# Memory key projection with 512-column products, its weights two rows to a chunk, first loads in halves, and four products on a zeroed tile ahead of it

## What is computed

```python
def memory_kv(mem, norm_mem, wk, wv, k_norm):
    mn = rms_norm(mem, norm_mem)
    k = rms_norm((mn @ wk).reshape(B, N_MEM, X_HEADS, X_HD), k_norm)
    v = (mn @ wv).reshape(B, N_MEM, X_HEADS, X_HD)
    return k, v
```

## Time and profile before

| | us |
|---|---|
| median of 3 runs | 1373.4 (1371.75 to 1374.05) |
| the profiled execution's own time | 1376.92 |
| its span on the core | 1375.1 |
| PE, DVE, ACT, POOL busy in the span | 1339.6, 828.0, 612.3, 119.8 |

### The profile page before, as it was taken

One profiled execution on the slowest core, in us unless ns is written; L12 is line 12 of the kernel. 1 busy time (PEld: TensorE's weight loads), 2 busy tenths in 40 slices (PEclk: granted clock), 3 DMA queues, 4 the chain that ended last, 5 costly groups with the idle time before them and its releaser, 6 DMA issues.

```text
span 1375.1 us, 27283 instructions
## 1 busy us (share of the span) xinstructions
PE 1339.6 (97%) x10211; PEld 1309.1 (95%) x10211; DVE 828.0 (60%) x1256; ACT 612.3 (45%) x865; POOL 119.8 (9%) x165
## 2 busy tenths in 40 slices
PE   7999999989999999999999999999999999999999
PEld 7998989877999988999999999999999999999999
DVE  7767888767666557856544555544555544565443
ACT  7674656465544454544333334333333333343332
POOL 0040000111322215400000000000000000000000
PEclk9999999988999999999999999999999999999999
DMA  9686444754864963654555455554455544545553
GB/s 380 254 240 223 133 136 136 221 176 138 304 234 158 283 238 123 195 171 154 168 168 168 153 173 164 168 167 164 151 174 168 167 161 162 164 155 181 162 162 128
DMA packets 75277, 251.88 MB, mean 183 GB/s; under 512 B 8332, under 2 KB 17376, under 8 KB 74560
## 3 DMA queue, kind: packets, MB, share of 16 engines
q1 hardware_dynamic: 59184, 215.49, 47.1%
q0 software_dynamic: 15744, 35.07, 8.1%
q10 hardware_dynamic: 288, 0.48, 0.1%
HBM read 238.00 MB, written 13.63 MB: 183 GB/s over the span
## 4 chain that ended last, share of the span: by engine, by line
PE 78%; DVE 11%; ACT 5%; issue 4%; DMA 2%; SPq 0%; DVEq 0%; ACTq 0%
PE g L514 74%; DVE arena L1434 4%; PE m L514 3%; ACT arena L981 2%; DMA raw<-in_stream 2%; DVE wlo L1448 2%; DVE arena L1431 2%; ACT whi L999 1%; DVE a_lo L1434 1%; DVE b_lo L1434 0%; DVE small L1714 0%; ACT a_hi L981 0%; DMA arena<-in_memT 0%; DVE small L1431 0%; PE m L739 0%
## 5 line engine op out<-in xcount | busy, mean ns | idle before, releaser
L1448 DVE TENSOR_TENSOR wlo<-raw,whi 128x1024 fp32r<-128x1024 f32 x388 | 477.7, 1241 | 371.9 <-ACT whi L999 360.2
L999 ACT ACTIVATE whi<-raw 128x1024 fp32r<-128x1024 f32 x388 | 407.6, 1058 | 479.1 <-PE g L514 439.4
L514 PE MATMUL g<-a_hi,whi 128*128 128x288 f32 x1632 | 355.6, 299 | 0.9 <-ACT a_hi L981 0.9
L514 PE MATMUL g<-a_hi,wlo 128*128 128x288 f32 x1632 | 351.1, 296 | 0.0
L514 PE MATMUL g<-a_lo,whi 128*128 128x288 f32 x1632 | 349.8, 296 | 0.0
L514 PE MATMUL g<-b_hi,whi 128*128 128x288 f32 x1344 | 287.3, 295 | 2.8 <-DVE arena L1431 2.7
L514 PE MATMUL g<-b_hi,wlo 128*128 128x288 f32 x1344 | 288.7, 296 | 0.0
L514 PE MATMUL g<-b_lo,whi 128*128 128x288 f32 x1344 | 286.8, 295 | 0.0
L514 PEld LDWEIGHTS g<-a_hi,whi 128*128 128x128 f32 x1632 | 263.6, 189 | 7.8 <-issue 4.8
L514 PEld LDWEIGHTS g<-a_lo,whi 128*128 128x128 f32 x1632 | 263.4, 189 | 0.0
L514 PEld LDWEIGHTS g<-a_hi,wlo 128*128 128x128 f32 x1632 | 262.7, 189 | 0.0
(11 more groups left out here) (181 smaller groups left out, 722.9 us busy)
## 6 DMA issues: line engine op xcount, KB each, us to landing
raw<-in_stream SPq DMA_DIRECT2D x388, 512.0 KB, 3.5
arena<-in_state_C POOLq DMA_DIRECT2D x8, 512.0 KB, 6.9
out_s_C<-arena POOLq DMA_DIRECT2D x8, 512.0 KB, 3.4
arena<-in_kdT POOLq DMA_DIRECT2D x8, 512.0 KB, 17.1
arena<-in_cache_mem_v POOLq DMA_DIRECT2D x8, 512.0 KB, 7.9
arena<-in_xT SPq DMA_DIRECT2D x4, 576.0 KB, 8.5
arena<-in_xT POOLq DMA_DIRECT2D x1, 2304.0 KB, 10.3
arena<-in_memT SPq DMA_DIRECT2D x4, 512.0 KB, 7.2
```

Of the source, the lines that this page charges most:

```text
L514: return pe.matmul(out, lhsT, rhs, start=start, stop=stop, skip_group_check=True)
L999: act.activation(whi[:, s], raw[:, s], ACT.Copy).then_inc(sem["hi_done"], 1)
L1448: dve.tensor_tensor(wlo[:, s], raw[:, s], f32(whi[:, s]), SUB).then_inc(sem["chunk_split"], 1)
```

## The change

`weight_stream` gives the eight memory key chunks another shape: chunk c holds two tiles of 128 rows (kt = 2c, 2c+1) with all 512 columns. `mem_chunk` runs them: two row tiles, three products, two tiles of 128 tokens, so 12 matmuls of 512 columns; the sums of all eight chunks stay in G[2] and G[3]. memT is loaded in eighths, five of them ahead of chunk 4 and three behind chunks 4 to 6. Chunk 0 is loaded and split in two halves with signals of their own. `mem_prep` and `x_prep` move to other chunks: `mem_prep` pairs beside chunks 0 to 4, `x_prep` pairs beside chunks 3 to 10. `warm` runs four products of `rstd` with itself, which DVE has just set to zero. DVE empties the memory keys after beside[7], in four copies of 256 columns. `chunk` itself, with its wait for `tile_out`, is not edited. In the diff a line "..." marks what is left out.

```diff
     every = range(0, D, CK * P)
-    out = tiles(w["wk_x"][0], every, range(0, XW, CW))
+    out = [w["wk_x"][0][r:r + 2 * P].reshape(2, P, 2, CW).transpose(0, 2, 1, 3).reshape(CK * P, CW)
+           for r in range(0, D, 2 * P)]
     out += tiles(w["w_in"][0], every, (COL_KA,))
...
-            for b in range(4):
+            def mem(b):
+                load(memT[:, 2 * b:2 * b + 2, :], ins["memT"][:, 2 * b:2 * b + 2, :], sem["mem_in"][b])
+
+            half = 2 * CW
+            load(raw[:, 0, 0:2].rearrange("p a b -> p (a b)"), ins["stream"][0][:, 0:half], sem["raw_ready"][0])
+            mem(0)
+            load(raw[:, 0, 2:4].rearrange("p a b -> p (a b)"), ins["stream"][0][:, half:2 * half], sem["first_raw"])
+            for b in range(1, 4):
                 chunk(b, ins["stream"][b], None)
-                load(memT[:, CK * b:CK * b + CK, :], ins["memT"][:, CK * b:CK * b + CK, :], sem["mem_in"][b])
+                mem(b)
+            mem(4)
             for b in range(4):
                 chunk(b, ins["stream"][RING + b], b + 1)
+                if b < 3:
+                    mem(5 + b)
                 load(xT[:, CK * b:CK * b + CK, :], ins["xT"][:, CK * b:CK * b + CK, :], sem["x_in"][b])
...
         beside = {c: [] for c in range(4 * WOUT)}
-        for kt in range(12, KT):
-            beside[0].append(("mem_prep", kt))
+        for kt in range(6, KT):
+            beside[kt // 2 - 3].append(("mem_prep", kt))
         for kt in range(KT):
-            beside[2 + kt // 2].append(("x_prep", kt))
+            beside[3 + kt // 2].append(("x_prep", kt))
         beside[7].append(("gate_weights",))
...
+            def warm():
+
+                pe.wait_ge(sem["dve_once"], before["warm_ready"] + 1)
+                for _ in range(4):
+                    mm(M[3][:, 0:256], rstd[:, 0:P], rstd[:, 0:256])
+
+            def mem_chunk(c):
+
+                if c:
+                    pe.wait_ge(sem["chunk_split"], c + 1)
+                s = c % RING
+                for k in range(2):
+                    kt = 2 * c + k
+                    if c == 0:
+                        pe.wait_ge(sem["first_hi"] if k == 0 else sem["hi_done"], 1)
+                    pe.wait_ge(sem["mem_hi"], kt + 1)
+                    for i, (w, a) in enumerate(((whi, act_hi[1]), (whi, act_lo[1]), (wlo, act_hi[1]))):
+                        if i == 1:
+                            pe.wait_ge(sem["mem_lo"], kt + 1)
+                        if i == 2 and c == 0:
+                            pe.wait_ge(sem["first_lo"] if k == 0 else sem["chunk_split"], 1)
+                        for j in range(2):
+                            m = mm(G[2 + j][:, :], a[:, kt, j * P:(j + 1) * P],
+                                   w[:, s, 2 * k:2 * k + 2, :].rearrange("p a b -> p (a b)"), kt == 0 and i == 0,
+                                   kt == KT - 1 and i == 2)
+                            if kt == KT - 1 and i == 2 and j == 0:
+                                m.then_inc(sem["tile0_done"], 2)
+                m.then_inc(sem["chunk_used"], 1)
+
             def chunk(c, t, src, first=True, last=True, tokens=False, more_c=0, more_t=0, kt0=0, each=None):
...
+            warm()
             for c in range(4 * WOUT):
                 g = c // 4
-                each = ("mem_hi", "mem_lo") if g == 0 else ("x_hi", "x_lo") if g == KVA else None
-                chunk(c, 2 * g, 1 if g < KVA else 0, c % 4 == 0, c % 4 == 3, g < KVA, kt0=CK * (c % 4), each=each)
+                if g < KVA:
+                    mem_chunk(c)
+                else:
+                    chunk(c, 2 * g, 0, c % 4 == 0, c % 4 == 3, kt0=CK * (c % 4),
+                          each=("x_hi", "x_lo") if g == KVA else None)
                 for what in beside[c]:
...
             def mem_prep(kt):
-                act.wait_ge(sem["mem_in"][kt // CK], 16)
+                act.wait_ge(sem["mem_in"][kt // 2], 16)
                 A(act_hi[1][:, kt, 0:SEQ], memT[:, kt, :], scale=gcol[:, 16 + kt:17 + kt]).then_inc(sem["mem_hi"], 1)
...
-            for c in range(RING - 1):
+            act.wait_ge(sem["raw_ready"][0], 16)
+            act.activation(whi[:, 0, 0:2], raw[:, 0, 0:2], ACT.Copy).then_inc(sem["first_hi"], 1)
+            act.wait_ge(sem["par_in"], 16)
+            mem_prep(0)
+            act.wait_ge(sem["first_raw"], 16)
+            act.activation(whi[:, 0, 2:4], raw[:, 0, 2:4], ACT.Copy).then_inc(sem["hi_done"], 1)
+            mem_prep(1)
+            for c in range(1, RING - 1):
                 split(c)
-                if c == 0:
-                    act.wait_ge(sem["par_in"], 16)
-                for kt in range(CK * c, CK * c + CK):
+                for kt in range(2 * c, 2 * c + 2):
                     mem_prep(kt)
...
             dve.wait_ge(sem["dve_once"], now("eps_ready"))
+            dve.memset(rstd[:, :], 0.0).then_inc(sem["dve_once"], 1)
+            dve.wait_ge(sem["dve_once"], now("warm_ready"))
             dve.memset(sm_(TINY), 2e-35).then_inc(sem["dve_step"], 1)
...
-            for c in range(RING - 1):
+            dve.wait_ge(sem["first_hi"], 1)
+            dve.tensor_tensor(wlo[:, 0, 0:2], raw[:, 0, 0:2], f32(whi[:, 0, 0:2]), SUB).then_inc(sem["first_lo"], 1)
+            mem_prep(0)
+            dve.wait_ge(sem["hi_done"], 1)
+            dve.tensor_tensor(wlo[:, 0, 2:4], raw[:, 0, 2:4], f32(whi[:, 0, 2:4]), SUB).then_inc(sem["chunk_split"], 1)
+            mem_prep(1)
+            for c in range(1, RING - 1):
                 split(c)
-                for kt in range(CK * c, CK * c + CK):
+                for kt in range(2 * c, 2 * c + 2):
                     mem_prep(kt)
...
                         do[what[0]](*what[1:])
-                if c % 4 == 3 and c // 4 != KVA or c == 4 * KVA + 4:
+                if c == 4 * KVA - 1:
+                    for j in range(2):
+                        if j == 0:
+                            dve.wait_ge(sem["tile0_done"], 2)
+                        else:
+                            dve.wait_ge(sem["chunk_used"], 8)
+                        for half in range(2):
+                            copy(kvm[:, j, half * CW:(half + 1) * CW],
+                                 G[2 + j][:, half * CW:(half + 1) * CW]).then_inc(sem["tile_out"], 1)
+                            dve.wait_ge(sem["tile_out"], now("tile_out"))
+                elif c > 4 * KVA and c % 4 == 3 and c // 4 != KVA or c == 4 * KVA + 4:
                     q = c // 4 if c % 4 == 3 else KVA
...
                         g, t = G[(2 * q + j) % GB], 2 * q + j
-                        if q < KVA:
-                            copy(kvm[:, j, q * CW:(q + 1) * CW], g[:, 0:CW]).then_inc(sem["tile_out"], 1)
-                            dve.wait_ge(sem["tile_out"], now("tile_out"))
-                        elif QKM <= q < OM and (q - QKM) % 2 == 0:
+                        if QKM <= q < OM and (q - QKM) % 2 == 0:
                             ct = q - QKM + j
```

More of the change, by code:

```diff
@@ L203 @@
 w_exp wg_in xT_in x_exp x_hi x_lo x_max x_normed x_prob x_rt x_rT x_sq x_ss xo_hi xo_lo
-xo_mm xp_T xp_out xs_mm y_stored
+first_hi first_lo first_raw xo_mm xp_T xp_out xs_mm y_stored
 """
-SLOT_SIGNALS = dict(raw_ready=4, c_in=4, c_out=4, bt_in=2, rb_in=2, vdec_in=2, mv_in=4, mem_in=4, x_in=4, mtok_in=2, xtok_in=3)
+SLOT_SIGNALS = dict(raw_ready=4, c_in=4, c_out=4, bt_in=2, rb_in=2, vdec_in=2, mv_in=4, mem_in=8, x_in=4, mtok_in=2, xtok_in=3)
 ONCE = dict(
@@ L213 @@
                   da_hi=4, km_out=2, xd_exp=1, xdp_out=2, od_act=1),
-    dve_once=dict(eps_ready=1, wg_split=3, diag_ready=3, rstd_x=1, g_nz=1, g_exps=1, kdup_out=2, vtok_out=2, vrev_out=1,
+    dve_once=dict(eps_ready=1, warm_ready=1, wg_split=3, diag_ready=3, rstd_x=1, g_nz=1, g_exps=1, kdup_out=2, vtok_out=2, vrev_out=1,
                   gcols_out=5, rm_ready=1, memk_ready=8, qd_ready=4, qr_ready=3, d_max=1, dprob=1, dpn_out=1, da_lo=4, vm_ones=2, xd_max=1,
```

## The result

The changed kernel takes 1383.2 us (median of 4 runs, 1382.7 to 1383.5) where the kernel before takes 1373.7 (4 runs beside it): ratio 1.0058, 95% interval 1.0044 to 1.0073. It is slower, as forecast, but by 9.4 us instead of 5.3, and lies above the range.

A forecast was written before the change was run, and what follows sets the result against it. The prediction took TensorE, busy 97% of the span, to bound the kernel. A wait at chunk 8 (3.1 us) plus the clock (2.2) made 5.3 us, moving the median from 1373.4 to 1378.7; range 1374.0 to about 1381.5.

The forecast's parts named there:

- where it is decided: At chunk 8: its wait for tile_out in DVE's order moves its start from 33.15 to 37.75; 3.1 us lost at norm_x.
- the front is covered: Chunks 0 to 7: front ends at 29.8 instead of 33.15, but its 3.3 us gain lies ahead of chunk 8's wait.
- the extension of the rows by 0.015 per 32 columns: In the eight memory chunks: a 512-column matmul costs 0.232 us, extended from the 256- and 288-column rows.
- the landings: Weights of chunks 7 to 12 land as before: chunk 10 at 31.6, chunk 12 at 39.79.
- cost nothing while the DMA engines are full: Ahead of SP's first wait: ten load issues instead of eight cost nothing, with a backlog of several us behind them.
- the clock: Behind the gap ahead of chunk 8: matmuls at half clock lose 2.2 us, with ends of nothing and 2.8.
- The sum: Over the whole kernel: 3.1 us for the wait plus 2.2 for the clock, 5.3 us slower; chance 0.56.
- The first: At chunk 8: held but pays less, without a queue loss or clock fall; costs 1.6 to 3.1 us; chance 0.19.
- The second: At norm_x: transfers decide, TensorE waits there for the squares, 1.1 us later than before, 1374.5; chance 0.14.
- The third: At chunk 8: it starts when chunk 7 ends, at 29.8, everything 3.3 us earlier, 1370.1; chance 0.11.

The follow-up runs named there:

- e2: Changed kernel with SP's wait for the memory tiles moved from behind chunk 8's load to behind chunk 10's; 1380.8 us, ratio 1.0052 to the kernel before.
- e6: Kernel before, with chunk 8 waiting for four tile_out instead of two; 1379.5 us, ratio 1.0039 to the kernel before.
- e10: As e9, without the four zero products at the start; 1372.1 us, ratio 0.9981 to the kernel before.
- e7: Kernel before, with SP also waiting, behind chunk 8's load, until DVE has split eight chunks; 1379.5 us, ratio 1.0044 to the kernel before.
- e5: Changed kernel with 20 more zero products behind chunk 7, filling TensorE's gap ahead of chunk 8; 1382.2 us, ratio 1.0055 to the kernel before.
- e1: Changed kernel without TensorE's wait for tile_out at chunk 8; 1380.4 us, ratio 1.0045 to the kernel before.
- e4: Changed kernel with the edits of e3, x tiles one chunk earlier and squares beside chunks 8 to 10; 1374.2 us, ratio 0.9999 to the kernel before.
- e3: Changed kernel with both edits, no tile_out wait at chunk 8 and SP's wait later; 1376.6 us, ratio 1.0018 to the kernel before.
- e11: Kernel before, with only e9's order of x tiles, squares and memory-by-tokens loads; 1373.1 us, ratio 0.9989 to the kernel before.
- e9: As e4, with the memory by tokens loaded behind chunk 15; 1372.4 us, ratio 0.9989 to the kernel before.

## Why the prediction was right in its sign and wrong in its size

**Right: where it is decided.** Chunk 8 waits for `tile_out` in DVE's order, behind the split of chunk 10, two x tiles, the gate weights and two copies. e2 shows it near the forecast place in the changed kernel (38.17 against 37.75), e6 in the kernel before (37.77).

**Right: the front is covered.** It ended at 30.6 (29.8 forecast). A 512-column matmul cost 16.6/72 = 0.231 us, as the extension of the rows by 0.015 per 32 columns said (0.232). The Trainium skill's rule (TensorE: Matmul & The Clock Gate, section Back-to-back issue gap), columns at 2.4 GHz and 2.5 ns, makes it an estimated 0.216; the trace does not agree. The section gives that rule for one matmul by itself and sets it apart from a stream of loads and matmuls, which the prediction did not say. The first product started 2.6 us earlier, at 5.30, and the zero products changed nothing (e10).

**Wrong: the landings.** The step that failed is "SP still issues each load several us before its turn; so I keep these landings". It counted the bytes ahead of chunks 7 to 12, and the backlog at SP's first issues, but not SP's own wait for the sixteenth memory tile behind chunk 8's load. The change delays that tile from 19.2 to 28.4 us. SP stood 11.0 us, the queue ran dry, chunk 10 landed at 35.8 instead of 31.6, and chunk 8 started at 41.07 instead of 37.75: 3.3 us. Of these, 2.9 go when SP's wait is moved (e2). The other 0.4 fit a second sentence that failed, though no run takes them apart, that ten issues instead of eight "cost nothing while the DMA engines are full": from 5.0 to 7.8 us they were not, with 301 GB/s instead of 405. e7 shows that SP's wait alone is worth as much as the one that the forecast found.

**Sized a little low: the clock.** 2.2 us were taken from the start of the kernel; chunks 8 to 12 took 2.7 longer, with 5.8 us at 0.50 instead of the 4.85 at the start. That the start was at this level is read from the matmuls' distance alone, since the earlier trace rows shows 1.00 for it. The term lay inside the ends given (0 to 2.8). e5 takes it away and gets 3.0 back, 0.3 of them from the earlier copies.

**The sum.** 5.3 forecast, of which 3.1 for the wait and 2.2 for the clock. With 2.9 for SP's wait, 0.4 for the rest of the late landing, 0.5 more for the clock and 0.4 for the wait at norm_x, 9.5, against 9.6 at norm_x and 9.4 in the median. That the median agrees so well is in part luck: other kernels here miss their position by 1 to 3 us (e1, e4, e7).

**The rivals.** The first did not come about: the fall of the clock came in full. The second (the transfers decide at norm_x) is what is left in e3, 2.3 us late instead of 1.1. The third, the gain kept, needed chunk 10 earlier; nothing made it earlier.

## What to carry to other kernels

Where work is spread out over more steps, look for every wait that counts that work, on all engines, the queues that issue transfers among them: a counter that used to be full long before anyone asked may now be asked first. A wait on a free buffer's turn is still a wait (e6: 5.5 us for two banks that nobody held), so a change that merges several results into one late emptying should come with its own look at who waits for the count. And a gain ahead of a transfer-bound stretch was worth nothing here until the order behind it was changed too (e3), and that order alone (e11) gave all that can be told from no change.

## What the runs showed of the hardware that was not expected

Gains and losses of a few us at 50 us do not come out one to one at the end. e5 reached norm_x 3.0 us before the changed kernel and ended 0.9 before it; e4 reached k_norm 1.4 us before the old kernel and ended 0.2 behind it. Behind chunk 13 TensorE's instructions are the same in all these kernels, yet in the profiles it took from chunk 13's start to the last matmul between 1312.1 us (e1) and 1316.7 (the kernel before). What differs with it is the clock. Windows of the kernel before:

```profile
250.00:340.00 90.00, 78.78 (x544) 68.08 (x543) 61.45 (x151) 48.79 (x95) 15.74 (x25) 0.89 0.61 190
```

and of e1:

```profile
250.00:340.00 90.00, 77.74 (x574) 66.98 (x573) 63.17 (x155) 49.29 (x96) 15.74 (x25) 0.96 0.63 196
```

The gaps of TensorE there (the earlier trace rows has two of them; the mean granted clock over all is 0.89 here and 0.96 there) are followed by a fall in one execution and not in another. Over the twelve profiles the two go together: the time at 0.50 from chunk 13 on, summed from windows of 1 us, lies between 6.8 us (e1, e9) and 24.1 (the kernel before), and the stretch grows by about 0.24 us with each us of it (correlation 0.91). Runs of one kernel show it too: beside e5, the kernel before took 1372.2 to 1372.5 us in three runs at a mean clock of 0.998 and 1374.3 to 1375.9 in four at 0.993. So a single profile's span can mislead by some us here: the profile of the kernel before ended 6.6 us ahead of the changed one's, where the medians are 9.4 apart. e5's profile has 20.6 us at 0.50 from chunk 13 on where the changed kernel's has 13.8, and takes 1.8 us longer there; that is what is missing of its 3.0 in the profiles. Why the falls come in one execution and not in another stays open, and whether the medians differ for the same reason is not shown.
